# Narrow f32 matmuls of two gates moved to four column groups of the TensorE array

## The reference, cut to what matters

```
q, k, v, g, gk_lr = jnp.split(h @ w_in, ...)          # gk_lr: 16 columns
log_a = jax.nn.log_sigmoid((gk_lr @ w_gk2 + b_gk).astype(jnp.float32)) / GLA_GATE_TAU
```

```
q = blockdiag(xc, wq)
k = blockdiag(xc, wk)
v = blockdiag(xm, wv)
gates = (jnp.concatenate([q, k, v], axis=-1) @ w_if + b_if).astype(f32)
log_i = gates[..., :H]
log_f = jax.nn.log_sigmoid(gates[..., H:])
```

## Time and profile before

| | us |
|---|---|
| three runs, median (lowest to highest) | 1945.14 (1944.67 to 1945.3) |
| the profiled execution, span from first to last instruction | 1943.5 |
| the profiled execution, own time | not listed apart from the three runs |
| TensorE busy | 1810.6 |
| GpSimd busy | 1225.6 |
| VectorE busy | 1158.3 |
| ScalarE busy | 952.8 |

### The profile page before, as it was taken

One profiled execution on the slowest core, in us unless ns is written; L12 is line 12 of the kernel. 1 busy time (PEld: TensorE's weight loads), 2 busy tenths in 40 slices (PEclk: granted clock), 3 DMA queues, 4 the chain that ended last, 5 costly groups with the idle time before them and its releaser, 6 DMA issues.

```text
span 1943.5 us, 29234 instructions
## 1 busy us (share of the span) xinstructions
PE 1810.6 (93%) x9848; PEld 1371.5 (71%) x9848; DVE 1158.3 (60%) x2484; ACT 952.8 (49%) x1765; POOL 1225.6 (63%) x708
## 2 busy tenths in 40 slices
PE   8999999999999999899999999999999887777877
PEld 7999888999999998789998878875544322222322
DVE  5444545444544468754456775576677666677664
ACT  5444646444544466654448444554444444444443
POOL 8888666888788877388887952534543344433431
PEclk9999999999999999999999999999999999999999
DMA  7555444655565554255554341499999999999997
GB/s 267 188 188 185 152 146 126 196 187 189 169 194 188 184 174 155 75 188 186 184 184 131 130 142 55 154 363 421 421 421 421 421 421 422 421 421 421 407 415 296
DMA packets 98266, 486.34 MB, mean 250 GB/s; under 512 B 11888, under 2 KB 12912, under 8 KB 65152
## 3 DMA queue, kind: packets, MB, share of 16 engines
q1 hardware_dynamic: 60304, 213.20, 34.6%
q0 software_dynamic: 36864, 268.45, 33.3%
q10 hardware_dynamic: 1008, 3.54, 0.5%
HBM read 484.10 MB, written 1.05 MB: 250 GB/s over the span
## 4 chain that ended last, share of the span: by engine, by line
PE 69%; DMA 17%; ACT 5%; DVE 5%; issue 3%; POOL 1%; DVEq 0%; ACTq 0%; POOLq 0%
DMA arena<-uv_tab,arena 17%; PE ps L826 16%; PE ps L2598 9%; PE ps L177 9%; PE ps L179 8%; PE ps L178 8%; PE ps L824 7%; DVE arena L2779 2%; ACT arena L2472 1%; PE ps L207 1%; PE ps L829 1%; PE ps L2543 1%; POOL split L552 1%; PE ps L208 1%; PE ps L1767 1%
## 5 line engine op out<-in xcount | busy, mean ns | idle before, releaser
L552 POOL TENSOR_TENSOR split<-raw,split 128x1024 fp32r<-128x1024 f32 x358 | 859.6, 2410 | 295.6 <-ACT split L227 290.8
L227 ACT ACTIVATE split<-raw 128x1024 fp32r<-128x1024 f32 x382 | 404.7, 1062 | 497.4 <-PE ps L179 264.9
L2598 PE MATMUL ps<-arena 128*128 128x512 f32 x1024 | 495.0, 618 | 103.0 <-ACT arena L2472 102.5
L2649 POOL DMA_INDIRECT arena<-uv_tab,arena x256 | 269.3, 1052 | 385.9 <-PE ps L2598 354.0
L826 PE MATMUL ps<-xs,split 128*128 128x512 f32 x1344 | 470.6, 393 | 0.0
L2598 PEld LDWEIGHTS ps<-arena 128*128 128x128 f32 x1024 | 182.2, 192 | 402.3 <-ACT arena L2472 249.0
L824 PE MATMUL ps<-xs,split 128*128 128x256 f32 x1176 | 328.5, 279 | 0.0
L826 PEld LDWEIGHTS ps<-xs,split 128*128 128x128 f32 x1344 | 247.0, 188 | 43.5
L824 PEld LDWEIGHTS ps<-xs,split 128*128 128x128 f32 x1176 | 221.1, 188 | 6.9
L2779 DVE CUSTOM_DVE_ANT_0 arena<-arena,raw 128x1024 f32<-128x1024 f32 x128 | 156.8, 1225 | 104.2 <-DMA arena<-uv_tab,arena 103.5
L2779 DVE CUSTOM_DVE_ANT_0 arena<-arena 128x1024 f32<-128x1024 f32 x128 | 157.0, 1226 | 93.8 <-DMA arena<-uv_tab,arena 92.7
(11 more groups left out here) (418 smaller groups left out, 2759.5 us busy)
## 6 DMA issues: line engine op xcount, KB each, us to landing
raw<-wstream SPq DMA_DIRECT2D x393, 512.0 KB, 3.5
over_split<-wstream SPq DMA_DIRECT2D x8, 512.0 KB, 7.4
arena<-uv_tab,arena POOLq DMA_INDIRECT x256, 15.1
arena<-small SPq DMA_DIRECT2D x1, 1195.0 KB
arena<-xT SPq DMA_DIRECT2D x1, 1024.0 KB, 6.3
arena<-keys ACTq DMA_DIRECT2D x1, 1024.0 KB, 6.7
arena<-rows ACTq DMA_DIRECT2D x1, 512.0 KB, 4.5
over_h<-wstream SPq DMA_DIRECT2D x1, 512.0 KB, 8.7
```

What stands on the lines that cost most here:

```text
L227: act.activation(parts_of(k, m)[0], raw_slot(k, m), ACT.Copy).then_inc(k.hi_done, 1)
L552: pool.tensor_tensor(lo, raw_slot(k, n), hi.bitcast(F32), ALU.subtract).then_inc(k.lo_done, 1)
L2598: last = pe.matmul(ps[:, banks[t][0] + i, :], diag[:, n % 4, :], ring[n % NS][:, D + i * 512:D + (i + 1) * 512], start=False, stop=ends, s ...
L2649: pool.indirect_dma_start(ring[n % NS], None, ins["uv_tab"], bass.IndirectOffsetOnAxis(ap=ids[:, b, s:s + 1], axis=0)).then_inc(k.px_in[n ...
```

## The change

In the gate loops chunk c goes to column group c mod 4: its output lies in partitions 32 (c mod 4) to 32 (c mod 4) + 31 of the bank, and 32 columns of weights are loaded, the 16 or 8 wanted and those that follow them in memory. Each group now sums two chunks (low-rank gate) or four (mLSTM). The parts of the four groups are summed by a matmul. For the low-rank gate that is the second product itself, whose weights `w_gk2` are now laid out four times, with zeros for the unwanted rows, 128 x 512; VectorE's multiplication covers 128 partitions. For the mLSTM a copy on ScalarE brings the bank's 128 partitions to `cs`, and a matmul with a folded identity (`k.fold`, 128 x 8) sums them into 8 partitions of the same bank; the bias follows. This matmul stands behind product 2, and the forget gate's behind product 7 where it stood behind product 5. `setup` clears 32 columns behind the gate weights and builds the folded identity on VectorE.

```diff
@@ -56,6 +56,7 @@
 RAW = 6
 SPLIT = 4
 BODY = 12
+GROUP = 32
 
 
 def packet_plan():
@@ -494,6 +495,13 @@
 
     for engine in (block.scalar, block.vector, block.tensor):
         engine(lambda e: e.wait_ge(k.consts_made, 1))
+
+    @block.vector
+    def _(dve):
+        k.dve(dve.memset(k.w_gate_end, 0.0))
+        k.dve(dve.tensor_reduce(k.fold, k.ident.rearrange("p (g j) -> p j g", g=P // GROUP)[:, 0:2 * ML_H, :], AX_X, ALU.add))
+        k.dve.settle(dve)
+
     all_end(k, block)
 
 
@@ -994,6 +1002,8 @@
 
     osq = k.arena.t[:, zb_at:zb_at + 2 * H * SEQ].rearrange("p (h t) -> p h t", h=H)
     rms = take(H, SEQ)
+    lr_at = SMALL["w_lr"][0]
+    lr_weights = k.small_all[:, lr_at:lr_at + DC * GLA_RANK + GROUP - GLA_RANK]
     wlr = sm["w_lr"].rearrange("p (c m) -> p c m", c=DC)
 
     tiles = Tiles(k, ["D"] * 20)
@@ -1078,10 +1088,10 @@
         last.then_inc(k.gla_wlr, 1)
         k.dve(dve.memset(st, 0.0))
         norm_rstd(k, dve, r)
-        dve.wait_ge(k.gla_pe, 1)
-        dve.tensor_tensor(lr[0:GLA_RANK, :], ps[0:GLA_RANK, 6, 0:SEQ], k.rstd[0:GLA_RANK, 0:SEQ], ALU.mult
+        dve.wait_ge(k.gla_pe, 4)
+        dve.tensor_tensor(lr, ps[:, 6, 0:SEQ], k.rstd[:, 0:SEQ], ALU.mult
                           ).then_inc(k.gla_lr, 1)
-        dve.wait_ge(k.gla_pe, 2)
+        dve.wait_ge(k.gla_pe, 5)
         for h in range(H):
             k.dve(dve.tensor_scalar(zb[:, h, :], ps[:, 6 + h // 2, (h % 2) * SEQ:(h % 2 + 1) * SEQ],
                                     sm["b_gk"][:, h:h + 1], None, ALU.add))
@@ -1206,14 +1216,17 @@
         pe.wait_ge(k.gla_wlr, 1)
         pe.wait_ge(k.x_copied, copies)
         for c in range(DC):
-            last = pe.matmul(ps[0:GLA_RANK, 6, 0:SEQ], wlr[:, c, :], x[:, c, :], start=(c == 0), stop=(c == DC - 1))
-        last.then_inc(k.gla_pe, 1)
+            lo, at = GROUP * (c % 4), c * GLA_RANK
+            last = pe.matmul(ps[lo:lo + GROUP, 6, 0:SEQ], lr_weights[:, at:at + GROUP], x[:, c, :],
+                             start=(c < 4), stop=(c >= 4), tile_position=(0, lo), skip_group_check=True)
+            if c >= 4:
+                last.then_inc(k.gla_pe, 1)
         tile(2)
 
         pe.wait_ge(k.gla_lr, 1)
         for h in range(H):
             last = pe.matmul(ps[:, 6 + h // 2, (h % 2) * SEQ:(h % 2 + 1) * SEQ],
-                             k.w_gk2[:, h * P:(h + 1) * P], lr[0:GLA_RANK, :], start=True, stop=True)
+                             k.w_gk2[:, h * P:(h + 1) * P], lr, start=True, stop=True)
         last.then_inc(k.gla_pe, 1)
         for n in range(3, 8):
             tile(n)
@@ -1912,7 +1925,9 @@
                 act.wait_ge(k.ml_vt, 2 * s + half + 1)
                 act.activation(vt[s][0:n, half * 512:(half + 1) * 512], ps[0:n, 4 + half, :], ACT.Copy).then_inc(k.ml_vtc, 1)
 
-        act.wait_ge(k.ml_gate, 1)
+        act.wait_ge(k.ml_gate, 4)
+        act.activation(cs, ps[:, 4, 0:TOK], ACT.Copy).then_inc(k.ml_act, 1)
+        act.wait_ge(k.ml_gate, 5)
         act.activation(g8[0:2 * ML_H, :], ps[0:2 * ML_H, 4, 0:TOK], ACT.Identity, bias=k.b_if[:, :]).then_inc(k.ml_act, 1)
         act.preload_act_table_set(EXP_AND_LN)
         for c in range(3):
@@ -2033,7 +2048,7 @@
             split(k, dve, j, y[:, j, :]).then_inc(k.s5_ys, 1)
         for c in range(4, DC):
             k_copied(c)
-        dve.wait_ge(k.ml_act, 2)
+        dve.wait_ge(k.ml_act, 3)
         k.dve(dve.scalar_tensor_tensor(out=gf[R, :], in0=gf[R, :], scalar=0.0, in1=az[R, :],
                                        op0=ALU.min, op1=ALU.subtract))
         k.dve.settle(dve)
@@ -2153,15 +2168,18 @@
             for c in range(DC):
                 if m == 0:
                     pe.wait_ge(k.ml_xc, c + 1)
-                last = pe.matmul(ps[0:2 * ML_H, 4, 0:TOK], k.w_gate[:, m, c, :], src(c), start=(m == 1 and c == 0),
-                                 stop=(m == 0 and c == DC - 1), skip_group_check=True)
+                lo = GROUP * (c % 4)
+                last = pe.matmul(ps[lo:lo + GROUP, 4, 0:TOK], k.w_gate_wide(m, c), src(c), start=(m == 1 and c < 4),
+                                 stop=(m == 0 and c >= 4), tile_position=(0, lo), skip_group_check=True)
+                if m == 0 and c >= 4:
+                    last.then_inc(k.ml_gate, 1)
             return last
 
         pe.wait_ge(k.w_gate_made, 1)
         pe.wait_ge(k.s5_bu_used, S5_C)
         gates(1, lambda c: k.xm[:, c, 3:3 + TOK])
         k.last_states()
-        gates(0, lambda c: xc[:, c, :]).then_inc(k.ml_gate, 1)
+        gates(0, lambda c: xc[:, c, :])
         pe.wait_ge(k.ml_bd, 3)
         for n in range(2 * DC):
             m, c = n % 2, n // 2
@@ -2172,8 +2190,11 @@
             elif n >= 4:
                 pe.wait_ge(k.ml_kc, (n - 4) // 2 + 1)
             pe.matmul(ps[:, n % 4, 0:TOK], bd_qk[:, m, c, :], xc[:, c, :], start=True, stop=True).then_inc(k.ml_qkv, 1)
-            if n == 5:
+            if n == 2:
                 pe.wait_ge(k.ml_act, 1)
+                pe.matmul(ps[0:2 * ML_H, 4, 0:TOK], k.fold, cs, start=True, stop=True).then_inc(k.ml_gate, 1)
+            if n == 7:
+                pe.wait_ge(k.ml_act, 2)
                 pe.wait_ge(k.s5_y, 4)
                 pe.matmul(gf[R, :], k.ident[0:2 * ML_H, ML_H:2 * ML_H], g8[0:2 * ML_H, :], start=True, stop=True
                           ).then_inc(k.ml_gf, 1)
@@ -2862,7 +2883,7 @@
         k.raw = ctx.enter_context(nc.sbuf_tensor("raw", [P, RAW, D], F32))
         k.ps = ctx.enter_context(nc.psum_tensor("ps", [P, 8, 512], F32))
         k.zero_bf = ctx.enter_context(nc.sbuf_tensor("zero_bf", [P, 512], BF16))[:, :]
-        k.w_gk2 = ctx.enter_context(nc.sbuf_tensor("w_gk2_sb", [GLA_RANK, GLA_H * P], F32))
+        k.w_gk2 = ctx.enter_context(nc.sbuf_tensor("w_gk2_sb", [P, GLA_H * P], F32))
         k.b_if = ctx.enter_context(nc.sbuf_tensor("b_if_sb", [2 * ML_H, 1], F32))
         k.query_in = [ctx.enter_context(nc.semaphore(f"query_in{j}")) for j in range(10)]
         with ExitStack() as parts:
@@ -2909,7 +2930,10 @@
             (k.w_gk2[:, :], ins["w_gk2"]),
             (k.b_if[:, :], ins["b_if"]),
         ]
-        k.w_gate = take(2, DC, 2 * ML_H)
+        w_gate = take(2 * DC * 2 * ML_H + GROUP)
+        k.w_gate, k.w_gate_end = w_gate[:, 0:2 * DC * 2 * ML_H].rearrange("p (m c o) -> p m c o", m=2, c=DC), w_gate[:, 2 * DC * 2 * ML_H:]
+        k.w_gate_wide = lambda m, c: w_gate[:, (m * DC + c) * 2 * ML_H:(m * DC + c) * 2 * ML_H + GROUP]
+        k.fold = take(2 * ML_H)
         low = k.arena.at
 
         k.sq = take(DC, TOK)
@@ -3065,7 +3089,7 @@
         "wstream": wstream,
         "small": np.concatenate([small[n] for n in SMALL], 1),
         "xT": tokens(a["x"][0]), "metaT": tokens(a["meta_tokens_2"]),
-        "w_gk2": a["gla_w_gk2"][0], "b_if": a["ml_b_if_2"][0].reshape(2 * ML_H, 1),
+        "w_gk2": np.concatenate([np.pad(a["gla_w_gk2"][0], ((0, GROUP - GLA_RANK), (0, 0)))] * (P // GROUP)), "b_if": a["ml_b_if_2"][0].reshape(2 * ML_H, 1),
         "w_if": by_block(a["ml_w_if_2"][0]),
         "keys": keys, "rows": np.concatenate([a["norm2_g_2"][0], a["final_norm_g_2"]]).reshape(1, 2 * D),
         "uv_tab": np.concatenate([a["peer_u_2"][0], a["peer_v_2"][0]], 1),
```

## The result

The changed kernel takes 1950.53 us (median of 8 runs, 1949.03 to 1952.94) against 1944.91 before: a ratio of 1.003, 95% interval 1.002 to 1.0039. It is slower by about 5.6 us, where 1942.2 was forecast and 1944.3 was the upper end of the range. One of the eight runs of the kernel before took 2509.2 us and is left out of the ratio; the other seven lie between 1943.7 and 1945.63.

The account below looks back on a forecast made before the run. The chain of waits was put at 69% TensorE and 17% DMA, almost all of that the gathers. Terms of -2.6, -1.4, +0.2 and +0.9 sum to -2.9 from 1945.14, so 1942.2 us, range 1940.6 to 1944.3.

Parts of the forecast that it names:

- Four column groups run together: In the gate blocks, the four groups' matmuls overlap, so a block takes 0.93 to 0.98 us.
- the rival of groups in turn: Groups in the gate blocks do not overlap, so nothing is saved and new steps cost: +1.9, 1947 us; chance 0.06.
- Term 1: Low-rank gate in the linear attention: 2.6 us saved, with everything behind it moving along; bounds 0 and 2.6.
- The prediction's last sign of being wrong: The low-rank gate's 2.6 us given back at a later stage by a wait that did not move.
- Term 2: mLSTM gates: 1.4 us saved if the clock holds; bounds 0 and 5.3.
- Copy directly behind the last GELU: Sign of being right, mLSTM: ScalarE copies the gate parts right after its last GELU, which ends at 1158.50 us before the change.
- two idle stretches: mLSTM, around the sum of the gate parts: TensorE newly idles 2.3 and 1.7 us within 5.2.
- The 1.24 us stall gone: mLSTM: TensorE's 1.24 us idle before 1168.94, waiting for VectorE's splits, disappears.
- Term 4: mLSTM: new TensorE idle time drops the clock to half for about 3.4 us, costing 0.9 us; at most 1.7.
- the first rival: The clock stays at 1.00 through the mLSTM's two idle stretches: -3.8, 1941.3 us; chance 0.30.
- the row-by-row sum without a fall: mLSTM timing at full clock: the GLU starts near 1168.8 in place of 1170.22, 1.4 us earlier.
- Term 3: Start: two small VectorE setup steps before the stage barrier cost 0.2 us, between 0 and 0.4.

Follow-up runs that it names:

- e5_abs: The change in the linear attention alone, plus its absolute value taken on ScalarE instead of VectorE: 1941.60 us, ratio 0.9983 to the kernel before.
- e9_early: e3_ml with the arena moved 512 bytes in all, ScalarE's copy, bias and three query copies before the last GELU, forget gate back behind product 5: 1939.88 us.
- e3_ml: The kernel before with only the mLSTM part of the change, including its setup and 160-byte arena move: 1949.31 us, ratio 1.0021.
- e4_pad: The changed kernel with 88 more floats a partition, bringing the arena back to its old place modulo 512: 1944.92 us, ratio 1.0003 to the kernel before.
- e6_setup: e4_pad with the two VectorE setup steps moved to the head of the gate weights' making: 1944.78 us, ratio 1.0000 to the kernel before.
- e1_arena: The kernel before with only the arena's work buffers moved by 160 bytes a partition: 1949.14 us, ratio 1.0022.
- e2_gla: The kernel before with only the linear-attention part of the change, arena not moved: 1946.51 us, ratio 1.0007.

## Why the prediction was wrong, point by point

*Four column groups run together:* right. The gate blocks hold TensorE for 1.00, 0.95 and 1.03 us from their start to the next matmul's, against a forecast of 0.93 to 0.98 and the 1.16 set beside it, and the rival of groups in turn fell at the first block.

*Term 1, -2.6 us:* right up to the second product (2.64 won, VectorE's product with 1/rms on time as worked out), wrong behind it, at the step "Everything behind (bias, exponentials, next tiles) is released by this chain and moves with it". GpSimd's third subtraction did not move with it (213.49, where it was 213.48), and the absolute value slid under it: 1.8 us longer, then a fall of the clock. The place lost 0.57 in place of gaining 2.6. e5_abs shows it: with that step off VectorE the gain is there. The prediction's last sign of being wrong, a later wait that did not move, names this case, but no term or rival has a price for it.

*Term 2, -1.4 us if the clock holds:* the rows came as worked out up to the clock. Copy directly behind the last GELU, two idle stretches (2.52 and 1.07 us), the 1.24 us stall gone. With the 1.38 by which the block starts late, the first q copy was due at 1162.7 and came at 1163.05.

*Term 4, +0.9 us:* the fall came, so the first rival fell, but the term was mis-sized. The clock was at half not for 3.4 us but for 6.83, over the fold and products 3 to 7: 3.92 us for the last four products, which take 2.10 at full clock (eight records in e9_early). The GLU started 2.2 later than the row-by-row sum without a fall (1168.8 and 1.38). Terms 2 and 4 together were +0.8 and not -0.5. In e3_ml and e4_pad it was 6.83 again and the block lost 0.7; in e6_setup it was 3.41, the second idle stretch 1.62, and the block lost 0.14. What I called fixed, that "nothing in the change moves" the last GELU, was true and beside the point: the copy could stand ahead of it.

*Term 3, +0.2:* 0.69 in the profile, but the first normalisation moves by more than that between kernels without the two steps, with the moment of the clock's rise. What the steps cost is not shown.

*The step that failed most is not in the text.* The sum assumed that the gathers take as long as before. The move of the arena by 160 bytes was in the diff, `take` by `take`, and I gave it no term: 3.1 us in the profile of the changed kernel, 4.2 by e1_arena (2.5 to 6.0 by its interval), so about half of the loss or more. With it taken back (e4_pad) the changed kernel stands at 1944.92, still 2.7 above the forecast: that rest is the failed parts of terms 1 and 4, and what the start may have cost beyond 0.2. (In the single profile these parts are larger; it has the falls of the clock that it happened to have.) The rival on the slow side (groups in turn) had the wrong mechanism.

## What to carry to other kernels

An allocation is part of the cost of a change: where a later stage runs at the rate of its DMA, compare the places modulo 256 at which its buffers begin before and after, and pad. When a step comes earlier, look at what stands beside it at its new time, not only at what stands ahead of it: a VectorE step with two SBUF operands that slides under a GpSimd step takes its gain along. And a shorter product is worth nothing while its reader waits in order behind another wait on its own engine; with the groups, the order here decided between 0 and 5.5 us.

## What was not expected of the hardware

- Rows of 8 KB landing at 240 modulo 256 cost 2 ns of 312 each, at 208 1 ns, and at the places tried from 80 to 176 nothing, nor at 184 in the slot that stayed where it was. A start at a multiple of 256 itself was not tried.
- The same idle time does not always lower the clock. TensorE waited 2.31 to 2.33 us for the same scalings in the changed kernel, e2_gla and e4_pad; the clock fell behind it in the first two and stayed at 1.00 in the third. After 1.38 us of idle near 259 us it fell in the kernel before and held in e4_pad, e5_abs and e9_early. It held there in e1_arena too, whose rows come 1.6 us earlier against the kernel before from there on. So single profiles shift by that much against each other where the instructions are the same, and the medians of the runs decide. What else makes the clock fall is not shown.
- Not settled: why rows beginning at 80, 112, 128 and 176 modulo 256 run alike, how much of the 0.69 us at the start is setup, and why e4_pad gained more than the gathers lost.
